# A hybrid convolution and mixture-of-experts step: the front stage's order of work rewritten by hand on four engines, with more convolution taps on GpSimd

## The reference

```python
h = rmsnorm(x, g_mix[i])
z = h @ w_in[i]                                      # 1024 -> 1536 columns
a = z[..., :CONV_CH] * jax.nn.sigmoid(z[..., CONV_CH:2 * CONV_CH])
u = z[..., 2 * CONV_CH:]
c = silu(layernorm(causal_dwconv(a_ext, w_dw[i], b_dw[i]), g_conv_ln[i], b_conv_ln[i]))   # 31 taps, 512 channels
o_a = c @ w_pw[i] + b_pw[i]
o_b = multiscale_pool(u_ext, pos0, w_pool[i], pool_scale[i])        # windows of 2, 4, 8, 16 frames
x = x + jnp.concatenate([o_a, o_b], axis=-1) @ w_out[i]
h2 = rmsnorm(x, g_ffn[i])
```

## Time and profile before

| | |
|---|---|
| time, median of 3 runs | 1215.45 us (1213.06 to 1216.2) |
| the profiled execution's own time | 1214.85 us |
| its span (first to last instruction) | 1213.1 us |
| mean granted TensorE clock | 0.947 |
| PE busy | 1091.4 us (90%) |
| DVE, ACT, POOL busy | 524.6 us, 494.8 us, 240.2 us |
| front stage | from 0 to 456 us of the span |
| last z product ends | 192.8 us |

### The profile page before, as it was taken

The page is one execution under the profiler, slowest core; times in us unless marked ns, Lnnn a source line. Parts: engine busy times, 40 slices in busy tenths (PEclk is TensorE's granted clock), DMA queues, the critical chain, the costliest instruction groups (busy, mean ns, idle before and its releaser), DMA issues. The chain is left out here.

```text
span 1213.1 us, 17787 instructions
## 1 busy us (share of the span) xinstructions
PE 1091.4 (90%) x5269; PEld 628.3 (52%) x5270; DVE 524.6 (43%) x684; ACT 494.8 (41%) x666; POOL 240.2 (20%) x279
## 2 busy tenths in 40 slices
PE   3799995779859988699999999999999999969997
PEld 2699995657748764233333333333333333327885
DVE  4458895757742216212321321321321322256886
ACT  4433444444421215434534533543643544533333
POOL 1014474234520001110110110101101111022220
PEclk9899997878968987899999999999999999989999
DMA  6041833211201374899999999999999999974631
GB/s 217 11 121 52 242 85 139 70 41 70 88 18 52 127 270 181 317 397 387 339 398 396 361 398 394 366 398 394 365 396 396 363 396 397 400 298 154 230 139 40
DMA packets 149296, 300.31 MB, mean 248 GB/s; under 512 B 12032, under 2 KB 42784, under 8 KB 149259
## 3 DMA queue, kind: packets, MB, share of 16 engines
q1 hardware_dynamic: 134907, 264.69, 59.5%
q0 software_dynamic: 6512, 22.29, 5.3%
q10 hardware_dynamic: 7840, 12.85, 2.8%
HBM read 261.72 MB, written 38.06 MB: 247 GB/s over the span
## 5 line engine op out<-in xcount | busy, mean ns | idle before, releaser
L1776 PE MATMUL ps_gate_up<-weights,x_turned 128*64 128x512 f32 x1568 | 349.6, 598 | 1.4 <-issue 0.7
L106 ACT COPY weights<-raw_weights 128x2048 f32 (+1 forms) x99 | 186.0, 1899 | 100.6 <-issue 44.4
L1776 PEld LDWEIGHTS ps_gate_up<-weights,x_turned 128*64 128x64 f32 x1568 | 109.5, 137 | 206.9 <-issue 205.8
L106 DVE COPY weights<-raw_weights 128x2048 f32 x93 | 114.3, 1230 | 219.7 <-PE ps_gate_up L1776 79.9
L1789 PE MATMUL ps_y<-weights,h_turned 128*64 128x512 f32 x784 | 179.0, 598 | 0.9 <-ACT h_turned L1696 0.9
L780 DVE SCALAR_TENSOR_TENSOR taps_bank<-a_ext,par,taps_bank 128x640 f32<-128x640 f32 (+1 forms) x152 | 119.7, 788 | 4.0
L1736 DVE TENSOR_TENSOR hidden<-ps_gate_up,act_gate 128x256 f32<-128x256 f32 x49 | 20.8, 425 | 220.6 <-ACT act_gate L1687 208.6
L421 POOL TENSOR_TENSOR conv_pool_taps<-conv_pool_taps,tap_product 128x640 f32<-128x640 f32 (+1 forms) x64 | 91.6, 1432 | 63.5 <-ACT tap_product L511 57.5
L1789 PEld LDWEIGHTS ps_y<-weights,h_turned 128*64 128x64 f32 x784 | 52.2, 136 | 93.3 <-issue 92.2
L115 POOL COPY token_ids<-item_tokens 128x1 int32 (+1 forms) x48 | 8.7, 181 | 448.1 <-PE ps_x L1763 448.1
L511 ACT ACTIVATE tap_product<-a_ext,par 128x640 f32<-128x640 f32 (+1 forms) x80 | 58.1, 745 | 41.4 <-POOL conv_pool_taps L421 27.5
(11 more groups left out here) (285 smaller groups left out, 1573.4 us busy)
## 6 DMA issues: line engine op xcount, KB each, us to landing
raw_weights<-w_exp_gate SPq DMA_DIRECT2D x128, 512.0 KB
raw_weights<-w_exp_up SPq DMA_DIRECT2D x128, 512.0 KB
raw_weights<-w_exp_down SPq DMA_DIRECT2D x64, 1024.0 KB, 11.7
y_rows<-y_tile ACTq DMA_DIRECT2D x98, 128.0 KB, 5.4
y_rows<-zero_rows SPq DMA_DIRECT2D x16, 512.0 KB, 6.2
x_rows<-x_tile SPq DMA_DIRECT2D x9, 512.0 KB, 2.6
h_rows<-h_tile SPq DMA_DIRECT2D x9, 512.0 KB, 2.9
mixer<-x_rows SPq DMA_DIRECT2D x9, 512.0 KB, 4.6
```

The lines of the kernel that those rows point to most:

```text
L106: copy(S.work[s][:, :], raw).then_inc(S.w_ready[s], 1)
L1776: last = pe.matmul(ps_gu[side[j], :, :], x_t[:, c, side[of]], w[:, :, share(D_EXP, j)], start=(k == 0), stop=(k == KD - 1))
```

## The change

**Sizes.** `POOL_TAPS` goes from 10 for all units to 12 for v = 0 to 3 and 14 for v = 4 to 7, so DVE does 19 and 17 taps instead of 21. `TAPS_BEFORE`, `ADDS_BEFORE`, `STEPS_BEFORE` and `next_tap` count through the uneven units; the waits stay those of the same operations.

**Waits.** `o_to_hi(1, 0, ...)` on ACT now waits for `wo_split` 2, whose buffer lies over the raw output weights of the first half. `silu(m)` is split in `silu(m, c)`. `mean_products` carries the wait on `conv_done` itself, 4 for groups 0 to 2 and 8 for groups 3 and 4.

**Order.** The lists of ACT, DVE, POOL and (from the first mean on) PE are written out call by call. SP's list is not changed, and neither is a single instruction's shape, except that there are 24 more products and adds and 24 fewer taps. The parts that matter below (a line of "..." leaves lines out):

```diff
-POOL_TAPS = 10
-VEC_TAPS = TAPS - POOL_TAPS
+POOL_TAPS = (12,) * KC + (14,) * KC
+VEC_TAPS = tuple(TAPS - n for n in POOL_TAPS)
+TAPS_BEFORE = tuple(sum(POOL_TAPS[:v]) for v in range(2 * KC))
+ADDS_BEFORE = tuple(sum(POOL_TAPS[:v]) - v for v in range(2 * KC))
+STEPS_BEFORE = tuple(sum(VEC_TAPS[:v]) - v for v in range(2 * KC))
+
+def next_tap(count, of):
+    for v, n in enumerate(of):
+        if count < n:
+            return v, count
+        count -= n
...
@@ POOL
-                add_taps(KC * POOL_TAPS)
+                add_taps(54)
                 ln_pow(0)
-                add_taps(5)
+                add_taps(7)
                 ln_pow(1)
+                add_taps(10)
                 rms_pow(0)
-                add_taps(10)
+                add_taps(12)
+                ln_pow(2)
+                add_taps(8)
                 rms_pow(1)
-                ln_pow(2)
-                add_taps(5)
-                rms_pow(2)
-                add_taps(9)
-                rms_pow(3)
-                add_taps(11)
+                add_taps(13)
...
@@ ACT, first part: gates and us of a block now stand behind products
                 gates(0, 1)
-                gates(0, 2)
+                products(1)
                 split_w(1, "g")
                 split_w(1, "a")
-                for n in range(CHUNKS):
-                    us(0, n)
-                    products(1)
-                u_tail(0)
+                gates(0, 2)
+                products(2)
+                us(0, 0)
+                products(2)
+                us(0, 1)
+                products(3)
+                gates(1, 0)
+                us(0, 2)
                 split_w(1, "u")
...
@@ ACT, from the last z product on
-                conv_square(0)
-                silu(0)
+                products(5)
                 o_to_hi(0, 0, 2)
                 w_out_hi(0)
-                o_to_hi(0, 2, 4)
+                conv_square(0)
                 w_out_hi(1)
-                o_to_hi(0, 4, BLOCKS)
+                o_to_hi(0, 2, 3)
+                products(1)
+                w_out_hi(2)
+                silu(0, 0)
+                a_tail(3)
+                silu(0, 1)
+                silu(0, 2)
+                silu(0, 3)
+                w_out_hi(3)
+                o_to_hi(0, 3, 5)
+                products(2)
+                o_to_hi(0, 5, 6)
+                conv_square(1)
...
@@ DVE, around the last z product
+                split_w(3, "u")
+                taps(1)
+                window(2, 0)
...
+                window(2, 3)
                 taps(12)
-                split_w(3, "u")
-                windows(2)
-                taps(5)
+                window(3, 0)
+                window(3, 1)
+                window(3, 2)
                 gated(3, 2)
-                history(3)
-                taps(4)
+                window(3, 3)
                 centre(0)
...
@@ DVE, group 1
+                variance(1)
+                taps(3)
+                diagonals(1)
+                taps(4)
                 add(0, 0)
+                scale(1)
+                taps(1)
+                o_to_lo(1, 0)
+                o_to_lo(1, 1)
+                taps(4)
+                add(0, 1)
+                taps(3)
+                o_to_lo(1, 2)
                 taps(2)
...
@@ DVE, the last taps
+                o_to_lo(2, 5)
+                taps(5)
+                o_to_lo(2, 6)
+                taps(3)
+                add(2, 0)
+                add(2, 1)
+                o_to_lo(2, 7)
...
@@ PE
-                pe.wait_ge(conv_done, KC)
                 mean_products(0)
+                pe.wait_ge(S.mix_w_loaded, 32)
+                pe.wait_ge(a_ready, KC * CHUNKS - 1)
+                o_products(0, 0, 2)
                 var_products(0)
+                o_products(0, 2, 3)
                 broadcast(0)
+                mean_products(1)
+                o_products(0, 3, 8)
...
+                var_products(1)
                 out_products(0, 0)
+                broadcast(1)
+                o_products(1, 0, 2)
                 out_products(0, 1)
-                broadcast(1)
...
+                o_products(1, 2, 8)
+                turn2(0, 0)
+                mean_products(2)
+                out_products(1, 0)
+                turn2(0, 1)
+                var_products(2)
+                out_products(1, 1)
+                broadcast(2)
+                o_products(2, 0, 2)
+                route(0)
+                out_products(2, 0)
+                o_products(2, 2, 8)
+                turn2(1, 0)
+                out_products(2, 1)
+                turn2(1, 1)
+                route(1)
+                mean_products(3)
+                out_products(3, 0)
...
```

More of the change, by code:

```diff
@@ L937, in norm2 @@
                        .then_inc(h2_ready, 1)
-                centre(0)
-                window(3, 0)
-                variance(0)
-                window(3, 1)
-                diagonals(0)
-                scale(0)
-                dve.wait_ge(row_loaded, 80)
-                window(3, 2)
+                dve.wait_ge(inv_step, 1)
+                for g in range(POOL_GROUPS):
+                    dve.tensor_scalar(inv[:, g, :], count[:, :], float(2 << g), None, ALU.min).then_inc(inv_step, 1)
@@ new lines, in _ @@
+                mean(1)
+                take_lo(0)
+                norm(1)
+                split_w(0, "g")
+                take_lo(1)
+                mean(2)
+                split_w(0, "a")
+                take_lo(2)
+                norm(2)
+                take_lo(3)
+                take_lo(4)
+                mean(3)
+                split_w(0, "u")
+                take_lo(5)
+                norm(3)
+                take_lo(6)
+                take_lo(7)
+                take_lo(8)
@@ L956, in _ @@
-                w_out_lo(1)
-                centre(1)
-                w_out_lo(2)
-                w_out_lo(3)
-                add(0, 0)
-                variance(1)
+                diagonals(0)
+                taps(1)
+                scale(0)
+                w_out_lo(1)
+                w_out_lo(2)
+                centre(1)
+                o_to_lo(0, 3)
+                o_to_lo(0, 4)
+                w_out_lo(3)
+                o_to_lo(0, 5)
+                taps(2)
+                o_to_lo(0, 6)
@@ L1007, in _ @@
-                mean_square(TILES - 1)
-                norm2(TILES - 1)
+                o_to_lo(1, 3)
+                taps(2)
+                o_to_lo(1, 4)
+                dve.wait_ge(row_loaded, 80)
+                norm2(0)
+                o_to_lo(1, 5)
+                taps(2)
+                o_to_lo(1, 6)
+                taps(1)
+                o_to_lo(1, 7)
+                centre(2)
+                taps(9)
+                variance(2)
+                taps(4)
+                diagonals(2)
@@ new lines, in _ @@
+                taps(1)
+                add(1, 0)
+                add(1, 1)
+                scale(2)
+                taps(4)
+                o_to_lo(2, 0)
+                taps(1)
+                mean_square(1)
+                o_to_lo(2, 1)
+                taps(3)
+                o_to_lo(2, 2)
+                taps(1)
+                o_to_lo(2, 3)
+                norm2(1)
+                o_to_lo(2, 4)
+                taps(1)
+                o_to_lo(2, 5)
+                taps(5)
+                o_to_lo(2, 6)
@@ new lines, in _ @@
+                taps(3)
+                add(2, 0)
+                add(2, 1)
+                o_to_lo(2, 7)
+                mean_square(2)
+                norm2(2)
+                centre(3)
+                variance(3)
+                add(3, 0)
+                diagonals(3)
+                add(3, 1)
+                scale(3)
+                o_to_lo(3, 0)
+                mean_square(3)
+                o_to_lo(3, 1)
+                add(4, 0)
+                o_to_lo(3, 2)
+                norm2(3)
@@ new lines, in _ @@
+                o_to_lo(3, 3)
+                o_to_lo(3, 4)
+                o_to_lo(3, 5)
+                o_to_lo(3, 6)
+                add(4, 1)
+                o_to_lo(3, 7)
+                mean_square(4)
+                norm2(4)
+                centre(4)
+                variance(4)
+                add(5, 0)
+                diagonals(4)
+                scale(4)
+                add(5, 1)
+                mean_square(5)
+                o_to_lo(4, 0)
+                o_to_lo(4, 1)
@@ new lines, in _ @@
+                out_products(2, 0)
[6 more added lines that the diff above has]
+                out_products(3, 0)
+                turn2(2, 0)
+                turn2(2, 1)
+                var_products(3)
+                out_products(3, 1)
+                broadcast(3)
+                o_products(3, 0, 2)
+                route(2)
+                out_products(4, 0)
@@ new lines, in _ @@
+                o_products(3, 2, 8)
+                turn2(3, 0)
+                out_products(4, 1)
+                turn2(3, 1)
+                route(3)
```

(11 more changed lines are left out.)

520 lines of the change are left out of this document (262 added, 258 removed).

## The result

The changed kernel takes 1168.59 us (median of 4 runs, 1167.64 to 1170.24) against 1215.83 for the kernel before beside it: a ratio of 0.9616, with a 95% interval of 0.9596 to 0.9637. The forecast was 1173.0, with a range of 1158 to 1196. The profiled execution took 1167.64 us, with a span of 1165.9 against 1213.1.

The account below looks back on a forecast made before the run. The convolution and each group's norm chain, not PE's work, were taken to set the end. Terms summed to -46.8 us, plus 5 for what the schedule omits: -41.8 against 1214.85 gives 1173.0 us, range 1158 to 1196.

Parts of the forecast that it names:

- Up to the last z product: The stretch before 192.8 us: a split-weights wait goes, a bank wait may come; change 0, bounds +-2 us.
- Window 1: First 29.6 us after z: the 6.24 us wait goes, but the output weights' landing holds the square; change +0.6 us.
- Window 2: The next 40.2 us: the 12.11 us wait for o_to_lo goes, leaving 25.3 us; change -14.9 us.
- Window 3: Third window after z, a group of two tiles: falls from 48.8 to 42.1 us, change -6.7.
- Windows 4 and 5: Fourth and fifth windows together: fall from 66.6 to 42.1 us, change -24.5, if mean 3 needn't wait.
- Window 7: Seventh of the eight windows: gets a route from window 8 and one turn; change +1.6 us.
- The gate: At mean 3: conv_done 8 near 286, VectorE's taps 282, PE arriving 288.7 us; PE the bound again, but barely.
- The 5 us allowance: 5 us added for one or two 1.6 us clock dips and some 3 us of VectorE work held up by GpSimd.
- The hand-over rival: Second half: new lists leave 2.0 us a GpSimd operation, conv_done 8 at 312; gain 23.5, 1191 us; chance 0.20.
- The slower rival: GpSimd becomes the bound at conv_done 8, deciding from 2.4 us an operation; 1232 us; chance 0.06.
- no change: The 13 and 12 us waits turn up again at o_left or a z-part gates block; 1215 stays; chance 0.03.
- The better case: Waits go in all windows but 1 and 8, clock stays up: gain 57.9, 1157 us; chance 0.08.

Follow-up runs that it names:

- y3: Changed kernel with ScalarE's and VectorE's lists up to the last z product put back in the old order, the rest new: 1186.95 us, ratio 0.977.
- x4: Changed kernel with 8 of 31 taps a unit left out on VectorE in columns 640 to 1087 (output differs): 1168.25 us, ratio 0.9613.
- x2: Changed kernel's new order with the old split of taps (10 of each unit on GpSimd, 21 on VectorE): 1172.43 us, ratio 0.9636.
- y5: Changed kernel with GpSimd taking 12 of 31 taps in both halves instead of 12 and 14: 1170.3 us, ratio 0.9636.
- x1: Kernel before, old order of work, with the new split of taps (12 and 14 on GpSimd): 1227.87 us, ratio 1.0094.
- y6: Changed kernel with GpSimd taking 14 of 31 taps in both halves instead of 12 and 14: 1175.7 us, ratio 0.9685.
- y4: Changed kernel with four ScalarE products moved from ahead of us(3, 0) to behind it, leaving GpSimd nothing to add during window 2's sums: 1168.16 us, ratio 0.9618.
- y7: Changed kernel with group 0's norm pulled ahead and the output weights' low parts shrunk on VectorE (output differs): 1169.98 us, ratio 0.9618.
- y1: Changed kernel with conv_square(0) put ahead of w_out_hi(0) in ScalarE's list: 1169.71 us, ratio 0.9619.

## Why the prediction was right, step by step

The mechanism and its place were right: order, not the amount of work, and PE's waits at the three places named. That the sum of the parts is exact to 0.2 us is luck in part, since terms that were 1.6, 1.0 and 1.3 us short met others that were 2.3 and 1.5 too long. The term for what the schedule leaves out was too large.

- **Up to the last z product** (0, bounds +-2): it ended at 191.90 instead of 192.8. The wait for split weights went, and a new one of 1.99 us came at 181.72 for `us(3, 0)`, behind `window(2, 3)`, drawn out by the adds.
- **Window 1** (+0.6): -1.7, 2.3 us better than forecast. The chain is the one I gave: weights issued at the end of z, landing at 5.2 to 12.3, `w_out_hi(0)` at 200.40 (201 in the forecast), the square at 202.21 (203). The output half came 27.9 us behind z instead of 30.2. "The earlier taps give nothing here" is right against the wait of 6.24 us, which the weights replace; but with the old z lists and the new split (y3) mean 0 waited 8.5 us and the second wait came on top.
- **Window 2** (-14.9): -13.3. PE is idle there for 3.5 us, 2.9 of them in waits for `o_to_lo`.
- **Window 3** (-6.7): -8.2. **Windows 4 and 5** (-24.5): -23.5, with one half at the low clock in it. **Window 6** (-2.5): -2.7. **Window 7** (+1.6): +2.9, again with one such half. **Window 8** (-0.4): -0.1.
- **The sum**: -46.8 forecast, -46.6 measured between the last z product and the last `route`. What lies before gave 0.9 more, what follows 0.3 less.
- **The gate**: `conv_done` 8 came at 285.6 (286 in the forecast), VectorE's last tap at 281.6 (282), mean 3 at 285.69 (288.7). The three lie close, as said. "PE is the bound again, but barely" holds for GpSimd, whose last operation PE waits 0.18 us for. For VectorE it was too cautious: in x4 less work on it moved mean 3 by only 1.2 us. In x2 and y5 more of it made no wait there, but z had ended 4.1 and 2.2 us later, so these two do not show how much room VectorE has.
- **The 5 us allowance**, +5, is the term of the sum that was mis-sized. It was put at 5 and was worth nothing in the balance. Both clock dips that it names came, 1.5 us each, in windows 4 and 7, where they account for the 1.0 and 1.3 us by which those windows missed their terms; but windows 1 and 3 ended 2.3 and 1.5 us shorter than summed and paid for them. Of the 3 us of VectorE work held up by GpSimd, the sums of window 3 were held (two in 4.26 us against 2.64), but `centre(0)` behind them ended at 199.3 and ScalarE was waiting for the weights until 200.40, so it did not reach PE; the low parts of the output weights took 2.29 us each, as in the kernel before. Without the term the forecast would have been 1168.0.

The windows view of the changed kernel, one output half at full clock and the two dips (compare):

```profile
226.94:232.77 5.83, 5.83 (x27) 4.84 (x26) 5.72 (x10) 4.88 (x10) 4.32 (x4) 1.00 0.39 150
296.56:303.92 7.36, 7.36 (x28) 5.91 (x28) 1.30 (x5) 0.00 (x0) 1.07 (x2) 0.77 0.00 0
368.39:375.71 7.32, 7.32 (x28) 5.84 (x28) 1.28 (x1) 0.00 (x0) 0.30 (x1) 0.77 0.18 72
```

**The rivals.** The hand-over rival needed 2.0 us a GpSimd operation in the second half: the last 48 took from 215.05 to 285.63, 1.47 us each with everything between them. GpSimd waited for ScalarE's products only 10.4 us in all between 191 and 345, 7.1 of them at once, where it had been 25.1. The slower rival needed 2.4 us: the last nine adds took 12.40 us, 1.38 each. The hand-over rival is real in the old order, though, as x1 shows (2.26 us an operation, slower by 0.9%), and y6 shows one that I had only touched in "no change": too many products for ScalarE in the z part. The better case, 1157, needed PE busy for 187.9 us and idle for 17.4. It was busy for 191.8, 3.9 more, by its dips, and idle for 24.8: windows 1 and 8 were as that case had them, and windows 2 to 7 still hold 8.0 us of waits.

**One reading.** "z products with no gap to speak of" ahead of 192.8 was wrong: PE is busy for only 162.1 us of that stretch, and 160.8 of the 191.9 in the changed kernel. The gaps lie early, in both kernels, and so cost the forecast nothing.

On contention, y4 shows 5.13 against 2.64 us for two sums, and 1.43 against 0.18 on 16 columns, while the taps, with one operand in PSUM, keep 0.91 at 640 columns beside adds. The side that the Trainium skill states (GPSIMD Engine Reference, Specifications; and SBUF — State Buffer, Who interferes with whom, which calls the shared port pair an exclusive lock) agrees with that. The held operations were on PE's path in one place, the 1.99 us wait at the end of z, and taking them off it (y4) gained nothing in the end.

## What to carry to other kernels

When several engines work on one chain by fixed lists, first ask where each one's part stands in its list, and only then who gets how much of it: here the order was worth some 43 us, while the new shares of work in the old order cost 13. Take the time out of VectorE's taps or put the work before the wait, one at a time, before believing which engine holds a gate; the engine that fills it last may be waiting for a third one's list. And when a wait at the head of a stage is taken away, look for the load or the bank that is due right behind it: in the first window, edits that removed a wait of 4 to 9 us gained none of it.

## What was not expected of the hardware

One program's executions scatter by up to 11 us (y7, 1164.32 to 1175.44), and in the profiles single blocks of products at a lower clock account for part of it. In y1 and y7 the same z block behind the same 1.99 us wait took 6.73 us at a granted clock of 0.74, where it took 5.23 at 1.00 in the changed kernel, and the first block of 448 columns took 7.42 (0.65 in y1) where it took 5.10 (1.00). Together that is 3.8 of the 5.2 us by which their z parts ended later. So a difference of 2 to 4 us between two variants' profiles is not to be read as their edit until such blocks are counted.
